# Sample attention of a hybrid decoder step: where round 1's memory rows lie, in which order round 1 is scored, and how page numbers are read

## The chip, the cores and the metric

The kernel runs on one core of a Trainium2 chip. The metric is the device time of one execution in microseconds (us), lower is better. A time stands for a kernel as the median of several runs. Engines are named as in the profile: PE is the tensor engine, PEld its weight loads, DVE the vector engine, ACT the scalar engine, POOL the GpSimd engine, SP the sync engine. SP, ACT and POOL also issue DMAs. A "q" behind an engine's name (SPq, ACTq, POOLq) stands for what its instruction sequencer does, DMA issues above all.

## What is computed

One step of a decoder layer runs over 512 prompt tokens and over 8 sample sequences of 4 new tokens each, which have 2048 past tokens in paged caches (pages of 128 tokens). Each branch of the sample attention reads a different store:

```
def sample_layer(x, cache_cmp, cache_slc, cache_win, cache_mem, pool_buf, page_table, p, rel_bias):
    ...
    full_c = jnp.concatenate([gather(cache_cmp), kvc], axis=1)
    full_s = jnp.concatenate([gather(cache_slc), kvs], axis=1)
    ...
    o_cmp, o_slc = nsa_global(q, pos, full_c, full_s, p, rel_bias)
    win_kv = jnp.concatenate([cache_win, kvw], axis=1)
    ...
    o_win = win_attention(q[:, None], pos[None, :], win_kv[:, None], kpos, rel_bias)[:, 0]
    o_nsa = nsa_combine(gn, o_cmp, o_slc, o_win)
    o_mem = mem_attention(qm, cache_mem)
    y = layer_tail(x, gb, o_pool, o_nsa, o_mem, p)
```

`gather` takes 16 pages of a sequence by its row of the page table; a page of one cache is 128 x 256 numbers of four bytes, 128 KB. The compressed branch gives the importance by which 16 of the 33 blocks of the selected branch are chosen. The prompt tokens pass through the same layer, and all tokens then pass a mixture of 32 experts.

## The kernel before, in words

The program is a row of phases. Each phase writes a separate instruction list for every engine (`with nc.Block()`); `phase_over()` puts a barrier of all engines behind it. Within a phase, engines wait for each other through semaphores, and each engine runs its list in the order written. Nothing is reordered by a scheduler.

1. The input projections of all tokens, to about 173 us.
2. The compress phase, to about 303 us. For each sample sequence s, PE multiplies the 16 pages of the compressed cache (`products(s, c)`), then makes blocks and turned keys (`blocks`, `keys`). Pages come by three issuers: SP 7 of them and ACT 3 (`load_sub`, each page through `load_page`, which reads the page number into a register and issues a DMA from there), POOL 6 (`gather_sub`, an indirect DMA that needs no register). `load_page` is line 457, its register load line 456, POOL's gather line 462. Between them PE computes five gate products that fill its time. At its end the selected pages of the first sequences are fetched already, SP's and POOL's part of them.
3. The sample attention, 304 to 382 us. The 8 sequences go in two rounds of four; the four sequences of a round lie side by side in the 128 rows of a PSUM bank. A round has kinds M (memory, 256 tokens), W_ (local window, 512 tokens), S (selected, 2048 tokens in four quarters q) and C (compressed). `BATCH` lists the score products in order, `score(n)` makes the n-th into bank n % 2, DVE adds biases and finds maxima (`quarter`, `window_max`, `memory_max`), ACT takes exponentials (`memory`, `window`, `selected`), PE turns the probabilities (`turn_memory`, `turn_window`, `turn_selected`) and multiplies them by values (`memory_rows`, `window_rows`, `selected_rows`). Those of memory put their product in a bank named "mv", those of the window "wv", those of the selected pages "sv".
4. The prompt attention, 383 to 497 us, then up-projections, the router, and the expert stage to the end.

Memory limits decide what can be loaded early. Round 0's memory rows lie in `mem_rows`, and so do round 1's memory rows (after round 0's were used), and after those round 1's window keys and values. SP waits for each: for "mv" of round 0, then loads round 1's memory; for "mv" of round 1, then loads round 1's windows. Selected pages of round 1's sequences 2 and 3 come into places that round 0's selected pages hold until "sv" of round 0. They are issued by SP, ACT and POOL (12, 8 and 12 pages); `owner` says which.

The order in BATCH before, and the semaphores behind which SP issues:

```
BATCH = [(0, M, 0), (0, W_, 0)] + [(0, S, q) for q in range(4)] + [(1, M, 0), (1, S, 0), (1, W_, 0)] + [(1, S, q) for q in (1, 2, 3)]
...
                filled(sp, 2, "mv", 0)
                for s in range(4):
                    load_memory(sp, 1, s)
...
                filled(sp, 3, "mv", 1)
                for s in range(4):
                    load_window(sp, 1, s)
```

Of the kernel before, what the change touches and what calls it, by code (L numbers as in the profile page):

```python
# [217 lines left out]
def build_program(nc, i, o, stop_after=99):  # L218

    ctx = ExitStack()  # L220
    with ctx:
# [242 lines left out]
        def load_sub(eng, s, pgs):  # L464

            for pg in pgs:
                load_page(eng, page_of(sub_buf(s), pg), "cache_cmp", s, pg, s_sub[s % 3])
# [572 lines left out]
        s_spill = sem("s_spill")  # L1040
        scr_hT = scratch("scr_hT", [128, KD * NTOK])
# [18 lines left out]
        def load_selected(eng, r, s, q, who=0):  # L1060
            for pg in range(4 * q, 4 * q + 4):
                if owner(r, s, pg) == who:
                    load_page(eng, selected_page(r, s, pg), "cache_slc", 4 * r + s, pg, s_cl[r][q])
# [39 lines left out]
        with nc.Block() as block:  # L1103
            @block.sync
            def _(sp):
# [48 lines left out]
            def _(act):  # L1154
# [33 lines left out]
                for s in range(NS):  # L1188
# [74 lines left out]
            def _(pe):  # L1263
# [80 lines left out]
                for c in range(2):  # L1344
# [21 lines left out]
        BATCH = [(0, M, 0), (0, W_, 0)] + [(0, S, q) for q in range(4)] + [(1, M, 0), (1, S, 0), (1, W_, 0)] + [(1, S, q) for q in (1, 2, 3)]  # L1366
# [10 lines left out]
                    + S_(4) + S_(5) + [(2, ("mv", 0)), (3, ("wv", 0))] + P_(0) + [(2, ("sv", 0))]  # L1377
                    + S_(6) + [(6, ("m", 1)), (3, ("mv", 1)), (6, ("o", 0)), (7, ("om", 0)), (5, ("om", 1))]
                    + S_(7) + S_(8) + S_(9) + WP_(1) + S_(10) + [(2, ("wv", 1))] + S_(11) + P_(1) + [(3, ("sv", 1)), (6, ("o", 1))])
# [22 lines left out]
        with nc.Block() as block:  # L1402
            @block.sync
            def _(sp):
# [6 lines left out]
                for s in range(4):  # L1411
                    load_memory(sp, 1, s)
# [29 lines left out]
            def _(act):  # L1442
# [64 lines left out]
                selected(0)  # L1507
                filled(act, 2, "sv", 0)
# [11 lines left out]
                window(1)  # L1520
                window_turned(1)
# [4 lines left out]
            def _(dve):  # L1526
# [165 lines left out]
                selected_turned(0)  # L1692
                selected_rows(0)
                mask_blocks(1)
                memory_max(1)
                memory_rows(1)
                quarter(7)
                window_max(1)
                quarter(9)
                window_turned(1)  # L1700
                quarter(10)
                window_rows(1)
                quarter(11)
# [5 lines left out]
            def _(pe):  # L1709
                rows_of_seq = [slice(32 * s, 32 * s + 32) for s in range(4)]  # L1710
                window_of = lambda r: mem_rows if r else win_rows
                pe.wait_ge(s_sc, 16 * 12)
# [1363 lines left out]
```

## Time and profile before

| what | value |
|---|---|
| median of 3 runs | 1854.88 us (1852.64 to 1856.59) |
| time of the profiled execution | 1856.81 us |
| its span, first to last instruction | 1854.8 us |
| mean granted PE clock over the span | 0.949 of full speed |
| PE busy | 1714.4 us, 92% of the span |
| DVE / ACT / POOL busy | 550.5 / 338.1 / 449.9 us |

A profile is one execution. "Busy" counts the time in which an engine works on an instruction; register, branch, semaphore and DMA-issuing instructions are not in it. The profiled execution is 1.93 us above the median of the three runs, so a difference found in the trace is to be put onto the median, and its own time is not the kernel's time.

### The profile page before, as it was taken

What the parts mean: (1) busy time and instruction counts of PE and PEld (TensorE: products, weight loads), DVE (VectorE), ACT (ScalarE), POOL (GpSimd) and SP (SyncE); (2) the same over time, 40 slices, a digit from 0 to 9 for tenths busy, and PEclk for the clock granted to TensorE, in tenths of its full rate; (3) what the DMA queues carried; (4) which work ended last, traced back from release to release, by engine and by line L of the source; (5) the groups of instructions that cost most, each with busy time, mean ns of one, the idle gap of its engine ahead of it and who ended that gap; (6) DMA issues with size and microseconds to landing.
All of it is one profiled execution on the core that took longest, in us unless ns stands there. A gap on an engine that the chain in (4) does not pass through costs nothing.

```text
span 1854.8 us, 40016 instructions
## 1 busy us (share of the span) xinstructions
PE 1714.4 (92%) x16080; PEld 953.3 (51%) x16080; DVE 550.5 (30%) x1391; ACT 338.1 (18%) x740; POOL 449.9 (24%) x520
## 2 busy tenths in 40 slices
PE   7998997679799999879999999999999999999992
PEld 3446785244478884534465754444444444444441
DVE  1333113446401113453232313231323232323235
ACT  3232112146400001101111111111111111111110
POOL 1122326647400006011212212221212222222220
PEclk9997997779999999879999999999999999999996
DMA  9534757850251103339999999999999999999986
GB/s 342 198 104 150 252 162 221 278 210 2 84 165 57 52 25 119 139 151 404 425 422 425 416 421 411 428 423 421 422 421 408 427 423 420 423 420 406 430 338 248
DMA packets 86641, 541.98 MB, mean 292 GB/s; under 512 B 19888, under 2 KB 44048, under 8 KB 73617
## 3 DMA queue, kind: packets, MB, share of 16 engines
q1 hardware_dynamic: 64809, 498.50, 66.8%
q0 software_dynamic: 14544, 32.03, 5.1%
q10 hardware_dynamic: 7232, 10.73, 1.8%
q8 instruction: 32, 0.52, 0.1%
q14 instruction: 24, 0.20, 0.0%
HBM read 523.39 MB, written 29.78 MB: 298 GB/s over the span
## 4 chain that ended last, share of the span: by engine, by line
PE 54%; DMA 1%; DVE 0%; issue 0%; SPq 0%; POOLq 0%; POOL 0%; ACT 0%
PE psum L2987 36%; PE psum L3013 18%; DMA arena<-y_of 1%; PE psum L2997 0%; DVE arena L2977 0%; SPq L2826 0%; SPq L2828 0%; DMA y_of<-arena 0%; DMA arena<-scr_h,arena 0%; DVE arena L2920 0%; POOL arena L2857 0%; POOLq L2788 0%; ACT arena L2906 0%; POOLq L2861 0%; POOLq L2857 0%
## 5 line engine op out<-in xcount | busy, mean ns | idle before, releaser
L2987 PE MATMUL psum<-arena 128*32 128x512 f32 x6144 | 668.2, 592 | 2.7 <-issue 2.7
L2987 PEld LDWEIGHTS psum<-arena 128*32 128x32 f32 x6144 | 234.4, 108 | 417.0 <-issue 413.3
L3013 PE MATMUL psum<-arena 128*32 128x256 f32 x6144 | 344.9, 378 | 0.0
L3013 PEld LDWEIGHTS psum<-arena 128*32 128x32 f32 x6144 | 236.0, 109 | 110.0 <-issue 9.6
L2942 DVE TENSOR_TENSOR arena<-psum,arena 128x512 f32<-128x512 f32 x96 | 66.5, 692 | 582.4 <-PE psum L2987 582.4
L2874 POOL DMA_INDIRECT y_of<-arena x96 | 97.0, 1011 | 476.2 <-ACT arena L2906 476.2
L2902 ACT ACTIVATE arena<-arena 128x256 f32<-128x256 f32 x96 | 40.1, 418 | 610.1 <-DVE arena L2944 610.1
L2618 PE MATMUL psum<-arena 128*128 128x272 f32 x608 | 144.3, 395 | 1.6 <-PEq L235 1.6
L2618 PEld LDWEIGHTS psum<-arena 128*128 128x128 f32 x608 | 116.1, 191 | 28.5 <-issue 3.3
L2853 POOL DMA_INDIRECT arena<-scr_h,arena x96 | 98.8, 1030 | 48.9 <-POOL arena L2849 28.2
L878 PE MATMUL psum<-arena 128*128 128x512 f32 (+1 forms) x256 | 97.4, 541 | 12.7 <-DMA arena<-in_w_tok 10.1
L2906 ACT ACTIVATE arena<-psum,arena 128x256 f32<-128x256 f32 x96 | 45.7, 476 | 245.7 <-PE psum L3013 245.7
L878 PEld LDWEIGHTS psum<-arena 128*128 128x128 f32 x256 | 46.1, 200 | 62.7 <-issue 60.6
L1984 POOL TENSOR_SCALAR arena<-arena 128x512 f32<-128x512 f32 (+3 forms) x64 | 68.5, 1085 | 20.0 <-DVE arena L2111 20.0
L462 POOL DMA_INDIRECT arena<-in_cache_slc,arena x60 | 59.2, 987 | 49.9 <-DMA scr_gate<-arena 26.2
L2444 DVE TENSOR_TENSOR arena<-psum,arena 128x544 f32<-128x544 f32 x24 | 17.4, 725 | 181.3 <-ACT arena L2417 174.6
L2849 POOL COPY arena<-arena 128x3 uint32 x32 | 6.1, 189 | 268.2 <-DMA y_of<-arena 238.1
L2920 DVE STREAM_TRANSPOSE arena<-arena 128x768 f32<-128x768 f32 x33 | 32.2, 977 | 120.5 <-DMA arena<-scr_h,arena 120.5
L2625 PE MATMUL psum<-arena 128*128 128x272 f32 x256 | 63.2, 398 | 3.6 <-DMA arena<-in_w_up 3.6
L462 POOL DMA_INDIRECT arena<-in_cache_cmp,arena x48 | 46.6, 970 | 76.1 <-PE psum L1298 33.8
L440 POOL CAST arena<-arena 32x8 bf16<-32x8 f32 (+1 forms) x6 | 6.2, 1033 | 240.7 <-DMA arena<-in_b_gu 219.8
L1298 PE MATMUL psum<-arena 128*128 128x256 f32 x256 | 61.2, 393 | 3.1 <-DVE arena L1232 3.1
(369 smaller groups left out, 1520.5 us busy)
## 6 DMA issues: line engine op xcount, KB each, us to landing
arena<-in_w_gu SPq DMA_DIRECT2D x64, 4096.0 KB, 15.1
arena<-in_w_down SPq DMA_DIRECT2D x32, 4096.0 KB, 14.5
arena<-in_w_gb SPq DMA_DIRECT2D x24, 512.0 KB, 4.5
arena<-y_of SPq DMA_DIRECT2D x8, 1024.0 KB, 15.3
arena<-in_cache_cmp SPq DMA_DIRECT2D x62, 128.0 KB, 3.1
arena<-in_cache_slc SPq DMA_DIRECT2D x60, 128.0 KB, 6.5
arena<-in_x_all SPq DMA_DIRECT2D x8, 512.0 KB, 11.3
arena<-in_w_tok SPq DMA_DIRECT2D x2, 2048.0 KB, 14.0
```

The lines of the kernel that those rows point to most:

```text
L462: pool.indirect_dma_start(dst, None, i[table], bass.IndirectOffsetOnAxis(page_row[:, at:at + 1], 0)).then_inc(sem, 16)
L878: mm = pe.matmul(bank(2 + c)[0:r, 0:b - a], dstT(n)[:, k], w_tok[:, k, a:b], start=(k == 0), stop=(k == KD - 1))
L1298: mm = pe.matmul(sum_bank(s, c)[:, 0:2 * n].rearrange("p (g b m) -> p g b m", g=2, b=PAGES), w_cmp[:, c, j], turned, start=(j == 0), stop= ...
L1984: ins = pool.tensor_scalar(rows, rows, c[:, g:g + 1], None, ALU.mult)
L2618: pe.matmul(bank(4 * s + h)[:, 0:HALF], w_gb[:, u % 6, k], hT[:, k, t], start=(k == 0), stop=(k == KD - 1))
L2625: mm = pe.matmul(bank(4 * s + 2 + h)[:, 0:HALF], w_up[:, k, 128 * c:128 * c + 128], oT_of(k)[:, t], start=(k == k0), stop=(k == k1 - 1))
L2853: pool.indirect_dma_start(xg[:, g], None, h_quarters, bass.IndirectOffsetOnAxis(row_from[:, g:g + 1], 0), bounds_check=4 * NTOK - 1, oob_i ...
L2874: pool.indirect_dma_start(y_quarters, bass.IndirectOffsetOnAxis(row_to[:, g:g + 1], 0), y_rows[:, g], None, bounds_check=4 * 1024 * TOPK - ...
L2906: act.activation(y_rows[:, g], dn_half(g), ACT.Copy, scale=cur_gate[:, g:g + 1]).then_inc(e_yc, 1)
L2942: dve.tensor_tensor(gu_c[:, g], gu_bank(g), bias_sb, ALU.add).then_inc(e_ba, 1)
L2987: mm = pe.matmul(gu_bank(g)[32 * j:32 * j + 32].rearrange("p (h n) -> p h n", h=2), xgT[:, g, 32 * k:32 * k + 32], gu_w(slot)[:, part, :, ...
L3013: mm = pe.matmul(dn_half(g)[32 * j:32 * j + 32], actT[:, g, 32 * k:32 * k + 32], dn_w(slot)[:, part, 256 * j:256 * j + 256], start=(k == 0 ...
```

## The change

There are four parts.

- Round 1's memory rows get a place of their own: `stripes`, the first 512 columns of each of 8 rows of 544 columns at `tail_base`, where the prompt's queries, memory queries and keys lie. Their prompt columns are first copied out to a scratch tensor in DRAM (`scr_q`, 2 MB, issued by SP in the compress phase behind the spill of `hT`), and are brought back by SP behind "mv" of round 1. PE waits for that (`s_q_again`) at the start of the prompt attention. The four memory loads themselves (2 MB) are issued by ACT near the end of the compress phase.
- With `mem_rows` free of round 1's memory, round 1's windows are loaded there behind "mv" of round 0.
- Round 1's order: memory and window first, then the four selected quarters. The parts on PE, DVE and ACT move with it. SP loads all of round 1's last selected pages behind "sv" of round 0 without a further wait.
- `load_page` becomes `load_pages`: the numbers of several pages are read with one register load. `owner` is changed so that SP's two pages of a group of four stand side by side.

```
-        def load_page(eng, dst, table, s, pg, sem):
-
-            at = PAGES * s + pg
-            first = eng.value_load(page_row[0:1, at:at + 1], min_val=0, max_val=n_rows - 128)
-            eng.dma_start(dst, i[table][bass.ds(first, 128)]).then_inc(sem, 16)
+        def first_rows_of(eng, s, pgs):
+
+            at = PAGES * s + pgs[0]
+            return nc.values_load_multi_w_load_instructions(page_row[0:1, at:at + len(pgs)], engines=[eng.engine],
+                                                            min_val=0, max_val=n_rows - 128)[1]
+
+        def load_pages(eng, dst_of, table, s, pgs, sem):
+
+            for pg, first in zip(pgs, first_rows_of(eng, s, pgs)):
+                eng.dma_start(dst_of(pg), i[table][bass.ds(first, 128)]).then_inc(sem, 16)
...
         def load_memory(sp, r, s):
-            sp.dma_start(mem_rows[:, s], i["cache_mem"][4 * r + s]
-                         ).then_inc(s_ml[s], 16)
+            dst = stripes[:, 2 * s:2 * s + 2] if r else mem_rows[:, s].rearrange("p (v c) -> p v c", v=2)
+            sp.dma_start(dst, i["cache_mem"][4 * r + s].rearrange("p (v c) -> p v c", v=2)).then_inc(s_ml[s], 16)
...
+        stripes = arena[:, tail_base:tail_base + 8 * NTOK].rearrange("p (k c) -> p k c", k=8)[:, :, 0:NP_TOK]
+        scr_q = scratch("scr_q", [128, 8, NP_TOK])
...
-                return (OF_SP, OF_ACT, OF_POOL, OF_POOL if pg // 4 % 2 else OF_SP)[pg % 4]
+                return ((OF_SP, OF_ACT, OF_POOL, OF_POOL) if pg // 4 % 2 else (OF_SP, OF_SP, OF_ACT, OF_POOL))[pg % 4]
...
                         sp.dma_start(scr_hT, hT.rearrange("p k t -> p (k t)")).then_inc(s_spill, 16)
+                        sp.dma_start(scr_q, stripes).then_inc(s_q_spill, 16)
...
+                act.wait_ge(s_q_spill, 16)
+                for n in range(4):
+                    load_memory(act, 1, n)
...
-        BATCH = [(0, M, 0), (0, W_, 0)] + [(0, S, q) for q in range(4)] + [(1, M, 0), (1, S, 0), (1, W_, 0)] + [(1, S, q) for q in (1, 2, 3)]
+        BATCH = [(0, M, 0), (0, W_, 0)] + [(0, S, q) for q in range(4)] + [(1, M, 0), (1, W_, 0)] + [(1, S, q) for q in range(4)]
...
                 filled(sp, 2, "mv", 0)
                 for s in range(4):
-                    load_memory(sp, 1, s)
+                    load_window(sp, 1, s)
                 filled(sp, 3, "wv", 0)
                 for q in range(4):
                     load_selected(sp, 1, 0, q)
                 filled(sp, 2, "sv", 0)
-                for s in range(2, 4):
-                    load_selected(sp, 1, s, 0)
-                filled(sp, 3, "mv", 1)
-                for s in range(4):
-                    load_window(sp, 1, s)
-                for q in range(1, 4):
+                for q in range(4):
                     for s in range(2, 4):
                         load_selected(sp, 1, s, q)
+                filled(sp, 3, "mv", 1)
+                sp.dma_start(stripes, scr_q).then_inc(s_q_again, 16)
...
                 selected(0)
+                memory(1)
+                window(1)
                 filled(act, 2, "sv", 0)
                 for q in range(2):
                     for s in range(2, 4):
                         load_selected(act, 1, s, q, OF_ACT)
-                memory(1)
                 memory_turned(1)
                 heads_out(0)
+                window_turned(1)
                 for q in range(2, 4):
...
             @block.tensor
             def _(pe):
+                pe.wait_ge(s_q_again, 16)
                 def queries(i_q):
```

ACT in the compress phase, behind the first sequence's blocks. In the kernel before, its list there reads as follows; lines 456 and 457 stand three times in all, once for each page, and line 1200 comes behind them.

```order
L1185 ACTIVATE arena<-psum,arena 64x2x127 x4
L456 TENSOR_LOAD arena
L456 ISA x2
L457 ISA
L457 DMA arena<-in_cache_cmp 128x256
L456 TENSOR_LOAD arena
```

The same place in the changed kernel:

```order
L1192 ACTIVATE arena<-psum,arena 64x2x127 x4
L456 TENSOR_LOAD arena
L456 ISA x6
L462 ISA
L462 DMA arena<-in_cache_cmp 128x256
L462 ISA
L462 DMA arena<-in_cache_cmp 128x256
L462 ISA
L462 DMA arena<-in_cache_cmp 128x256
L1207 DMA arena<-in_rel_bias 32x8 x4
```

One register load (TENSOR_LOAD) stands there now where three stood; the checks on the registers (ISA) and the DMAs are as many as before.

PE in the sample attention, from the turning of round 0's selected probabilities (line 1803) to the last score of round 1. Before: 1819 is `selected_rows(0)`, 1747 the memory score of round 1, 1784 and 1793 its turning and its values, 1847 and 1854 the turned rows, 1760 the window and selected scores, 1827 and 1840 `turn_window(1)` and `window_rows(1)`.

```order
L1803 MATMUL psum<-arena 128x128 x16
L1806 MATMUL psum<-arena 32x128
L1819 MATMUL psum<-arena 32x128 x68
L1747 MATMUL psum<-arena 32x256 x8
L1784 MATMUL psum<-arena 128x128 x2
L1793 MATMUL psum<-arena 32x256 x8
L1847 MATMUL psum<-arena 128x128
L1854 MATMUL psum<-arena 128x128 x4
L1760 MATMUL psum<-arena 32x512 x12
L1827 MATMUL psum<-arena 128x128 x4
L1830 MATMUL psum<-arena 32x128
L1760 MATMUL psum<-arena 32x512 x4
```

The same stretch in the changed kernel, where line 1753 is the memory score, 1825 `selected_rows(0)`, 1766 the window and selected scores:

```order
L1809 MATMUL psum<-arena 128x128 x16
L1812 MATMUL psum<-arena 32x128
L1753 MATMUL psum<-arena 32x256 x8
L1825 MATMUL psum<-arena 32x128 x68
L1766 MATMUL psum<-arena 32x512 x4
L1790 MATMUL psum<-arena 128x128 x2
L1799 MATMUL psum<-arena 32x256 x8
L1853 MATMUL psum<-arena 128x128
L1860 MATMUL psum<-arena 128x128 x4
L1833 MATMUL psum<-arena 128x128 x4
L1836 MATMUL psum<-arena 32x128
L1846 MATMUL psum<-arena 32x128 x20
```

The memory score moved ahead of `selected_rows(0)`, the window's score ahead of `turn_memory(1)`, and all four selected scores (line 1766 again, x16) now follow `window_rows(1)`.

ACT in the sample attention, behind the copies of round 0's turned probabilities. Before, it goes at once to the pages of round 1's sequences 2 and 3:

```order
L1443 ACTIVATE arena<-psum 128x512 x2
L456 TENSOR_LOAD arena
L456 ISA x2
L457 ISA
L457 DMA arena<-in_cache_slc 128x256
```

In the changed kernel three exponentials of round 1 stand ahead of them, memory (128x256) and window (128x512 and 128x32):

```order
L1450 ACTIVATE arena<-psum 128x512 x2
L1456 ACTIVATE arena<-psum,arena 128x256
L1456 ACTIVATE arena<-arena 128x512
L1456 ACTIVATE arena<-arena 128x32
L456 TENSOR_LOAD arena
L456 ISA x2
L462 ISA
L462 DMA arena<-in_cache_slc 128x256
```

ACT's first four late pages thus stand behind the window's exponential, and the other four behind `window_turned(1)`.

## Rows read from the trace of the kernel before

**Rows 1.** The page: share of the span of the chain that ended last, by engine.

```profile
PE 54%; DMA 1%; DVE 0%; issue 0%; SPq 0%; POOLq 0%; POOL 0%; ACT 0%
```

**Rows 2.** Timeline of PE, sample attention: start, duration, line, [idle before, released by].

```profile
330.76 0.42 PE L1793 MATMUL psum<-arena 128*32 128x256 f32 x4
...
335.72 4.05 PE L1819 MATMUL psum<-arena 128*32 128x128 f32 x136
343.65 1.94 PE L1747 MATMUL psum<-arena 128*32 128x256 f32 x16 [3.89 <-DMA arena<-in_cache_mem]
347.89 1.93 PE L1793 MATMUL psum<-arena 128*32 128x256 f32 x16 [0.47 <-ACT arena L1443]
...
350.02 1.30 PE L1854 MATMUL psum<-arena 128*128 128x128 f32 x4
...
361.31 1.93 PE L1760 MATMUL psum<-arena 128*32 128x512 f32 x8 [6.70 <-DMA arena<-in_win_kt]
...
368.44 1.07 PE L1760 MATMUL psum<-arena 128*32 128x512 f32 x8
...
380.86 0.33 PE L1847 MATMUL psum<-arena 128*128 128x128 f32 x1 [0.53 <-DVE arena L1658]
```

**Rows 3.** Timeline of SP's and ACT's sequencers and of ACT, sample attention.

```profile
332.05 2.28 SPq L1033 DMA_DIRECT2D arena<-in_cache_mem  x4
...
349.89 1.77 SPq L1045 DMA_DIRECT2D arena<-in_win_kt  x4
...
340.52 3.71 ACTq L457 DMA_DIRECT2D arena<-in_cache_slc  x4
...
350.95 3.77 ACTq L457 DMA_DIRECT2D arena<-in_cache_slc  x4
...
365.15 0.19 ACT L1449 ACTIVATION_READ_ACCUMULATOR arena<-arena 128x1 f32 x1
```

**Rows 4.** POOL's page gathers, 300 to 365 us: ns min/median/max, first and last start.

```profile
L462 POOL DMA_INDIRECT arena<-in_cache_slc,arena x44: 942/947/2197, 304.8 to 361.1; - x44
...
DMA to landing us min/median/max: 3.3/5.5/6.9
```

**Rows 5.** Line 457 on ACT, 350 to 355 us: issue to landing.

```profile
DMA to landing us min/median/max: 7.7/8.1/8.5
```

**Rows 6.** Stretches: busy of each engine, granted PE clock, DMA share, GB/s.

```profile
276.00:284.00 8.00, 8.00 (x42) 6.76 (x41) 1.04 (x4) 2.91 (x9) 3.78 (x4) 1.00 0.86 319
284.00:292.00 8.00, 6.94 (x55) 6.62 (x54) 2.04 (x8) 3.22 (x11) 6.12 (x7) 0.69 0.97 306
292.00:300.00 8.00, 5.46 (x29) 5.03 (x28) 0.99 (x4) 1.96 (x7) 5.24 (x6) 0.50 0.71 199
356.00:360.00 4.00, 0.00 (x0) 0.00 (x0) 0.00 (x0) 0.28 (x2) 3.02 (x4) 0.50 1.03 372
198.80:201.20 2.40, 2.40 (x7) 1.82 (x6) 0.00 (x0) 0.28 (x1) 1.78 (x2) 0.50 0.82 254
```

**Rows 7.** Timeline of ACT in the compress phase, 186 to 195 us.

```profile
186.26 2.53 ACTq L457 DMA_DIRECT2D arena<-in_cache_cmp  x3
...
194.72 0.96 ACT L1185 ACTIVATE arena<-psum,arena 64x254 f32<-64x254 f32 x2 [8.17 <-issue]
```

**Rows 8.** Timeline of PE in the compress phase: the wait, and the next gate product.

```profile
197.62 0.33 PE L1319 MATMUL psum<-arena 127*128 127x127 f32 x1 [4.22 <-DVE arena L1247]
197.78 9.19 PE L1327 MATMUL psum<-arena 128*128 128x272 f32 x32
...
230.06 7.50 PE L1327 MATMUL psum<-arena 128*128 128x272 f32 x32
```

**Rows 9.** Line 456 on ACT, 186 to 189.5 us: ns min/median/max.

```profile
L456 ACTq TENSOR_LOAD <-arena x2: 282/288/294, 186.7 to 187.7; - x2
```

**Rows 10.** Line 1103, the barrier behind the compress phase: ns, first and last start.

```profile
L1103 POOLq DRAIN  x1: 17126/17126/17126, 285.9 to 285.9; - x1
...
L1103 ACTq DRAIN  x1: 228/228/228, 300.4 to 300.4; - x1
```

More of the change, by code:

```diff
@@ L464, in load_sub @@
         def load_sub(eng, s, pgs):
-            for pg in pgs:
-                load_page(eng, page_of(sub_buf(s), pg), "cache_cmp", s, pg, s_sub[s % 3])
+            load_pages(eng, lambda pg: page_of(sub_buf(s), pg), "cache_cmp", s, pgs, s_sub[s % 3])
         def gather_sub(pool, s):
@@ L1060, in load_selected @@
         def load_selected(eng, r, s, q, who=0):
-            for pg in range(4 * q, 4 * q + 4):
-                if owner(r, s, pg) == who:
-                    load_page(eng, selected_page(r, s, pg), "cache_slc", 4 * r + s, pg, s_cl[r][q])
+            pgs = [pg for pg in range(4 * q, 4 * q + 4) if owner(r, s, pg) == who]
+            load_pages(eng, lambda pg: selected_page(r, s, pg), "cache_slc", 4 * r + s, pgs, s_cl[r][q])
         def gather_selected(pool, r, s, q):
@@ L1376, in build_program @@
                     + [(2, ("cv", 0)), (7, ("im", 0)), (3, ("cv", 1)), (7, ("im", 1))] + S_(2) + S_(3) + [(6, ("m", 0))] + WP_(0)
[L1377 to L1379 removed]
+                    + S_(4) + S_(5) + [(2, ("mv", 0)), (3, ("wv", 0))] + P_(0) + S_(6) + [(2, ("sv", 0))]
+                    + S_(7) + [(6, ("m", 1)), (3, ("mv", 1)), (6, ("o", 0)), (7, ("om", 0)), (5, ("om", 1))]
+                    + WP_(1) + [(2, ("wv", 1))] + S_(8) + S_(9) + S_(10) + S_(11) + P_(1) + [(3, ("sv", 1)), (6, ("o", 1))])
         use_no = {}
@@ L1519, in _ @@
                 memory_out(1)
-                window(1)
-                window_turned(1)
                 selected(1)
@@ L1692, in _ @@
                 selected_turned(0)
+                memory_max(1)
+                window_max(1)
                 selected_rows(0)
                 mask_blocks(1)
-                memory_max(1)
                 memory_rows(1)
-                quarter(7)
-                window_max(1)
-                quarter(9)
                 window_turned(1)
-                quarter(10)
                 window_rows(1)
-                quarter(11)
+                for n in range(8, 12):
+                    quarter(n)
                 selected_max(1)
@@ L1711, in _ @@
                 window_of = lambda r: mem_rows if r else win_rows
+                memory_of = lambda r, s, v: stripes[:, 2 * s + v] if r else mem_rows[:, s, 512 * v:512 * v + 512]
                 pe.wait_ge(s_sc, 16 * 12)
@@ L1746, in score @@
                             for s, rows in enumerate(rows_of_seq):
-                                mm = pe.matmul(bank(b)[rows, 0:MEM], qm_rows[:, mp, 4 * r + s], mem_rows[:, s, 256 * mp:256 * mp + 256],
+                                mm = pe.matmul(bank(b)[rows, 0:MEM], qm_rows[:, mp, 4 * r + s], memory_of(r, s, 0)[:, 256 * mp:256 * mp + 256],
                                                start=(mp == 0), stop=(mp == 1), tile_position=(0, 32 * s))
@@ L1792, in memory_rows @@
                         for s, rows in enumerate(rows_of_seq):
-                            mm = pe.matmul(bank(b)[rows, 0:256], pT_m[:, a, rows], mem_rows[:, s, 512 + 256 * a:768 + 256 * a],
+                            mm = pe.matmul(bank(b)[rows, 0:256], pT_m[:, a, rows], memory_of(r, s, 1)[:, 256 * a:256 * a + 256],
                                            start=(a == 0), stop=(a == 1), tile_position=(0, 32 * s))
@@ L1873, in _ @@
                 turn_selected(0)
+                score(6)
                 selected_rows(0)
-                score(6)
+                score(7)
                 turn_memory(1)
@@ L1880, in _ @@
                 turn_memory_rows(1)
-                score(7)
-                score(8)
-                score(9)
                 turn_window(1)
-                score(10)
                 window_rows(1)
-                score(11)
+                for n in range(8, 12):
+                    score(n)
                 turn_selected(1)
```

1 line of the change is left out of this document (added).

## The prediction

> **What bounds the kernel now.** I read the page's chain first [rows 1]: half of the span is PE's, and that is the expert stage, which the change doesn't touch. Whatever the change gains or loses arises before 382 us and is carried on as a shift of what follows, so I read PE's timeline over the two phases that it edits and asked at each gap what ended it.
>
> In the sample attention PE has two long waits for something that the change moves [rows 2]: 3.89 us for round 1's memory rows at 343.65 and 6.70 us for its windows at 361.31. Both follow from the single place: SP could issue memory only at 332.05 and windows only at 349.89 [rows 3]. That looks like 10 us to be had. It isn't, because a second chain runs under it. POOL issues 44 gathers from 304.8 to 361.1 us [rows 4], one every (361.1 − 304.8) / 43 = 1.31 us, so it hardly stops, and its last gather, which belongs to the last quarter, lands some 5.5 us after its start, at 366.6. The last score product begins at 368.44 [rows 2]. Removing the two waits can therefore bring that score forward by 1.8 us, and by 4.0 us if the last gather lands in the shortest 3.3 us. What follows the last score (maximum, exponential, turning, values, to 380.86) is the same work after the change.
>
> In the compress phase PE is the limit but for one gap: 4.22 us at 197.62 for DVE [rows 8], which stands behind ACT, and ACT is busy with DMA issues until 194.72 [rows 7]. The phase ends by POOL's drain at 285.9 + 17.1 = 303.1 us, while ACT is through at 300.6 [rows 10].
>
> **The change, part by part.**
>
> *One register load for several pages.* On ACT's path to the gap, three register loads become one. A load takes 288 ns [rows 9], so two fewer give 0.6 us. The other bound: three issues with their numbers take 2.53 us [rows 7], issues without numbers 1.77 / 4 = 0.44 us each [rows 3], so all that reading costs behind the first load is 2.53 − 1.32 = 1.2 us. The checks on each register stay, so I take 0.6. PE's gap shrinks by that, and the gate products, POOL's start and the barrier move forward with it. On SP the register loads have slack everywhere. In the sample attention ACT has one page per group, so nothing is saved there.
>
> The Trainium skill, "DMA: Bandwidth & Descriptors", section "Latency and other measured facts", gives a tensor_load a floor of about 600 ns; by it the two would save about 1.2 us and the sum would be 0.6 us better. The trace has 282 to 294 ns here, and I go by that.
>
> *The clock.* Behind the 4.22 us gap the granted clock is 0.50 (1.2 of 2.4 GHz) from 198.8 to 201.2 [rows 6], and that gate product takes 9.19 instead of 7.50 us [rows 8]. A gap of 3.6 us may or may not keep the upper level: 0 to 1.7 us. I take 0, since the gap stays nearer to the old one than to none.
>
> *Storing the prompt queries, 2 MB, at about 202 us.* SP issues it behind the spill of hT. The pages that follow on its queue are issued only after the next sequence's products, and PE shows no wait for a page there. I cost it at nothing.
>
> *Round 1's memory rows, 2 MB, at about 285 us on ACT.* Four issues at 0.44 us are 1.8 us on ACT just before its last copies. ACT is through 2.5 us before the barrier falls, so this is covered. The traffic is less harmless: the barrier waits for POOL's drain, which waits for the gathers to land. Between 276 and 300 us the DMA engines move 319, 306 and 199 GB/s, which is 6.6 MB in 24 us [rows 6]. With 2.1 MB more it is 8.7 MB, and at the 372 GB/s of 356 to 360 us this takes 23.4 us: no delay. By the shares instead (0.86, 0.97 and 0.71), 3.7 us are idle and the new loads need 2.1 / 0.372 = 5.6 us: 1.9 us of delay. If the gathers stood behind all of it, 5.6 us. I take 1.0, between the first two.
>
> *Windows instead of memory behind "mv" of round 0.* That bank is full at 330.76 + 0.42 = 331.2 us [rows 2]. SP, which arrived at 332.05 and saves some 12 register loads before it, is waiting by then. From the first memory issue to PE's start took 343.65 − 332.05 = 11.6 us [rows 2, 3]; four windows are as large, so PE scores them at 342.8. Meanwhile the memory score (1.07 us, as the score at 368.44) stands ahead of selected_rows(0), which ends at 335.72 + 1.07 + 4.05 = 340.8 instead of 339.8. SP's pages behind "sv" start a microsecond later, POOL's not, as its 12 last gathers only come to their turn at 361.1 − 11 × 1.31 = 346.7.
>
> *ACT's list.* Here the change adds a wait. ACT's eight late pages start at 340.52 and 350.95 now [rows 3]. In the new order the first four stand behind the window's exponential. From a window score's start to the end of its exponentials is 365.34 − 361.31 = 4.0 us [rows 2, 3], so ACT is free at 346.8; a register load and its checks take 0.7 us (from the pitch of 1.08 us in [rows 7]) and the four issues 3.7: 351.2. Then come the memory copy (0.4), memory_rows and the turned rows (347.89 to 351.32, 3.4 us [rows 2]) and the window's turning and copy (an estimate of 1.4 from the turned rows' 1.30): 356.4. The second four are issued from there, the last at about 360.5 us, ten microseconds later than before. Behind ACT's pages stand memory_turned(1) and heads_out(0), for which PE waits, but PE ends that chain before the pages are there.
>
> *The last score.* It needs POOL's last page (361.1 + 5.5 = 366.6) and ACT's last. ACT's pages landed 7.7 to 8.5 us after issue while the windows came in beside them [rows 5]; POOL's in 3.3 to 6.9 [rows 4]. At 360 us the restored queries (2 MB, issued behind SP's last page near 354) take the windows' place, but are nearly through. I take 6.5 us: 367.0, with bounds 364.4 and 369.0. The score lasts 1.07 us at the full clock (368.44) and 1.93 at half (361.31) [rows 2]; PE idles before it, so I take 1.5: it ends at 368.5 instead of 369.5. That is 1.0 us gained, within 4.0 gained and 1.4 lost.
>
> *Bringing the queries back.* Issued near 354 and as large as the windows, which took 361.31 − 349.89 = 11.4 us, they are there at about 365.5, against a need at 382. Nothing.
>
> **The sum.** −0.6 (register loads) + 1.0 (POOL's drain) − 1.0 (last score) = −0.6 us. From the profiled 1856.8 this is 1856.2. That execution is 1.9 above the median of the runs, so on their scale it is 1854.88 − 0.6 = 1854.3 us.
>
> **The rivals.**
>
> *Faster.* The clock stays up behind the shorter gap (1.7), the drain isn't delayed, and the last pages land in POOL's shortest time with PE at full clock (4.0): 0.6 + 1.7 + 4.0 = 6.3 us, 1848.6. Two of the three already give over 3.7 us. For it: there is 2 MB less between 332 and 360 us, where the engines are full (share 1.03). Against it: the restored queries put those 2 MB back before the last gather lands, and POOL's pace is unchanged.
>
> *Slower.* One mechanism, in the compress phase: the four memory loads take the DMA engines ahead of POOL's gathers, and the drain waits for all their 5.6 us. The balance is 5.6 − 0.6 − 1.0 = 4.0 us, 1858.9. It decides from a barrier 4.7 us later than now, at about 308 us. For it: the engines' share is 0.97 just where the loads start. Against it: it is 0.71 from 292 us on, so much of the delay is made good.
>
> The Trainium skill, "DMA: Bandwidth & Descriptors", section "Queues, rings and completion order", says that each DMA engine takes its queues in turn, a packet at a time; by that neither queue stands behind the other, and this rival would lose only a part of its 5.6 us. No row here shows the turns themselves.
>
> *No gain because ACT's pages become last.* They land at 369.0 and the score runs at half clock, so that it ends at 370.9 instead of 369.5: −0.6 + 1.0 + 1.4 = +1.8 us, 1856.7. This is the way in which the change wouldn't do what it says. It lies within the bound of no change.
>
> *The restored queries come late* and PE waits at the prompt attention's start. They would have to take 28 us instead of 11.4; one in a hundred, counted with slower.
>
> **How the numbers follow.** About 0.2% (3.7 us) is what a measurement can tell from no change. The forecast and the third rival lie within it: 0.58. Faster gets 0.26, as two separate uncertain terms can bring it; slower 0.16. The range from 1849.5 to 1859.0 reaches into both; the likeliest case's own range is 1852.5 to 1856.7.
>
> **What would show it.** Right: three pages on ACT at 186 us with one register load; the gap at 197.6 about 3.6 us; POOL's drain ending within 302.5 to 305; the window score of round 1 near 343; ACT's last late page near 360; the last two scores waiting for selected pages; PE starting the prompt attention without a wait. Wrong: a barrier at 308 us, a full clock at 199 us, or a last score before 365 or after 370.

## The result: 0.23% slower, and the profile after

| kernel | median of 10 runs (lowest to highest) |
|---|---|
| before | 1855.34 us (1852.64 to 1856.59) |
| changed | 1858.86 us (1856.69 to 1862.57) |

The ratio is 1.0023, 95% interval 1.0015 to 1.0031: 3.5 us on the medians. The time lies inside the range, but the forecast was no change, and it is slower. The profiled execution took 1860.03 us, its span 1858.2.

The phases, cut where the barrier lets SP go (line 235), in the first profiled execution of each kernel and in a second one of each (first two experiments):

| phase, us | before | again | changed | again |
|---|---|---|---|---|
| projections | 175.12 | 174.86 | 177.70 | 174.35 |
| compress | 128.97 | 127.51 | 129.86 | 131.65 |
| sample attention | 78.63 | 78.51 | 78.50 | 78.56 |
| prompt attention | 116.16 | 116.19 | 116.43 | 116.15 |

The 2.6 us more in the first phase of the changed kernel are those of one execution. PE's first 32 matmuls of line 940, in the timeline of the changed kernel and, below, of its second profile (which has 29 of them in this row):

```profile
154.90 6.83 PE L940 MATMUL psum<-arena 128*128 128x2 f32 x32
```

```profile
153.83 4.54 PE L940 MATMUL psum<-arena 128*128 128x2 f32 x29
```

Stretches of the first of these profiles (length, then busy us and count of PE, PEld, DVE, ACT, POOL; granted clock; DMA share; GB/s) show why:

```profile
152.00:154.00 2.00, 1.22 (x12) 0.77 (x10) 1.36 (x2) 1.38 (x10) 0.00 (x0) 1.00 0.00 1
155.00:157.00 2.00, 2.00 (x12) 2.00 (x11) 1.90 (x4) 0.39 (x1) 0.00 (x0) 0.50 0.00 0
```

The clock fell to 1.2 GHz under these matmuls there, and later in the second profile (0.70 of full speed over 155 to 157 us). Of 18 profiled executions of all kernels, 16 have a first phase of 174.3 to 175.2 us. The two long ones, this one and that of loads_alone below, both read page numbers jointly, as do 12 of the 16; the runs of loads_alone as a whole are no slower than the kernel before. That joint loads make an early fall more frequent is neither shown nor excluded.

**The compress barrier.** The lines that answer to [rows 10], POOL's and also PE's drain, and PE's in the kernel before:

```profile
L1109 POOLq DRAIN  x1: 18938/18938/18938, 287.6 to 287.6; - x1
...
L1109 PEldq DRAIN  x1: 365/365/365, 301.3 to 301.3; - x1
```

```profile
L1103 PEldq DRAIN  x1: 363/363/363, 300.0 to 300.0; - x1
```

POOL's drain takes 18.94 us instead of 17.13 and ends at 306.5, 5.2 us after PE's began; in the kernel before it was 3.1 us (300.0 to 303.1). The traffic, issue to landing of the DMAs from 278.6 to 307.6 us (the last number, us; KB each before it where it is known), and the DMA share (next to last) of the stretches that answer to [rows 6]:

```profile
arena<-in_cache_mem ACTq DMA_DIRECT2D x4, 512.0 KB, 10.0
...
arena<-in_cache_slc,arena POOLq DMA_INDIRECT x16, 6.0
```

```profile
279.50:287.50 8.00, 6.97 (x46) 5.97 (x45) 1.07 (x5) 2.89 (x8) 5.30 (x6) 1.00 1.02 370
287.50:295.50 8.00, 7.24 (x54) 7.02 (x53) 1.99 (x8) 2.40 (x10) 6.03 (x7) 0.72 1.05 362
295.50:303.50 8.00, 3.59 (x20) 3.02 (x19) 0.99 (x4) 1.53 (x6) 3.78 (x4) 0.50 0.94 313
```

The room that [rows 6] showed is used up, and POOL's gathers take 6.0 us to land. In the kernel before (276 to 306 us) it was 3.5:

```profile
arena<-in_cache_slc,arena POOLq DMA_INDIRECT x17, 3.5
```

POOL starts its gathers at the same pace in both, one every 1.25 us. From the end of its last one to the end of the drain it is 4.31 us in each of the nine profiles without memory loads beside them, the kernel before included, and 6.2 to 7.2 us in the nine with them. In all 18 the drain ends 2.7 to 3.0 us after the last packet of POOL's queue, so it is the landing that the drain waits for.

**The gap near 197 us.** ACT and PE (timelines), to set beside [rows 7, 8]. First ACT in the changed kernel:

```profile
188.60 1.33 ACTq L462 DMA_DIRECT2D arena<-in_cache_cmp  x3
...
193.40 2.69 ACTq L1210 DMA_DIRECT2D arena<-in_c_force  x1
...
196.68 0.96 ACT L1192 ACTIVATE arena<-psum,arena 64x254 f32<-64x254 f32 x2 [8.68 <-issue]
```

The issue of c_force in the kernel before, and PE's row in the changed one:

```profile
192.54 1.47 ACTq L1203 DMA_DIRECT2D arena<-in_c_force  x1
```

```profile
199.57 0.47 PE L1329 MATMUL psum<-arena 127*128 127x127 f32 x1 [4.72 <-DVE arena L1257]
199.84 8.74 PE L1337 MATMUL psum<-arena 128*128 128x272 f32 x32
```

ACT's three pages go out in 1.33 us instead of 2.53, but a later issue on the same engine, of c_force (a constant of 16.5 KB), takes 2.69 us (1.47 before), and PE's gap is not shorter but longer, 4.72 us.

**The sample attention.** PE's timeline, to set beside [rows 2] (this execution is 3.5 us later at the phase's start):

```profile
346.25 1.07 PE L1766 MATMUL psum<-arena 128*32 128x512 f32 x8 [1.95 <-DMA arena<-in_win_kt]
...
352.98 1.93 PE L1799 MATMUL psum<-arena 128*32 128x256 f32 x16 [5.30 <-ACT arena L1450]
...
363.37 0.40 PE L1836 MATMUL psum<-arena 128*32 128x128 f32 x1 [6.11 <-ACT arena L1504]
...
366.64 4.23 PE L1766 MATMUL psum<-arena 128*32 128x512 f32 x24
371.60 1.07 PE L1766 MATMUL psum<-arena 128*32 128x512 f32 x8 [0.73 <-DMA arena<-in_cache_slc,arena]
```

The two waits for memory rows and windows are gone but for 1.95 us. The time went into two new ones, 5.30 and 6.11 us, behind ACT's late pages. Three of the four selected scores then run without a wait, and the last waits 0.73 us (1.58 in the second profile) for a page that POOL gathered: it starts 64.0 us into the phase, against 64.4 before, where it followed PE's own work without a wait [rows 2]. POOL's gathers of this phase, to set beside [rows 4], have the same number and pace:

```profile
L467 POOL DMA_INDIRECT arena<-in_cache_slc,arena x44: 940/946/2337, 308.3 to 364.7; - x44
...
DMA to landing us min/median/max: 2.8/4.3/7.8
```

But the last one lands later. In the kernel before, the last two take, from start to landing:

```profile
DMA to landing us min/median/max: 5.4/5.5/5.5
```

In the changed kernel PE's wait for the last one ends 6.9 us after its start (364.7 to 371.60; 6.5 in the second profile). The restored queries, 2 MB, are under way beside it: issued at 359.81, they land 13.4 us later, and the DMA engines are full (share 1.04 to 1.05) until 370 us.

### The profile page after: what moved, and what is told of

Its sections match the earlier page's. It is cut to its first block, busy times and chain, and to the rows that moved or that the text cites. A ratio compares the mean times of both kernels' runs of the same rounds, so it can differ in the third digit from the quotient of the medians.

```text
span 1858.2 us, 39924 instructions
## 1 busy us (share of the span) xinstructions
PE 1715.0 (92%) x16080; PEld 992.7 (53%) x16080; DVE 548.6 (30%) x1391; ACT 337.5 (18%) x740; POOL 448.9 (24%) x520
## 4 chain that ended last, share of the span: by engine, by line
PE 54%; DMA 1%; DVE 0%; SPq 0%; issue 0%; ACT 0%; DVEq 0%; POOLq 0%
PE psum L2992 36%; PE psum L3018 18%; DMA arena<-y_of 1%; PE psum L3002 0%; PE psum L2352 0%; DVE arena L2982 0%; DMA y_of<-arena 0%; SPq L2831 0%; SPq L2833 0%; DVE arena L2925 0%; DVE arena L2345 0%; ACT arena L2911 0%; DVEq L2793 0%; POOLq L2883 0%; POOLq L2879 0%
## 5 line engine op out<-in xcount | busy, mean ns | idle before, releaser
L2992 PEld LDWEIGHTS psum<-arena 128*32 128x32 f32 x6144 | 261.1, 108 | 389.9 <-issue 375.4
L3018 PEld LDWEIGHTS psum<-arena 128*32 128x32 f32 x6144 | 246.7, 109 | 99.8 <-issue 8.8
```

Of the source, the lines that this page charges most:

```text
L2992: mm = pe.matmul(gu_bank(g)[32 * j:32 * j + 32].rearrange("p (h n) -> p h n", h=2), xgT[:, g, 32 * k:32 * k + 32], gu_w(slot)[:, part, :, ...
L3018: mm = pe.matmul(dn_half(g)[32 * j:32 * j + 32], actT[:, g, 32 * k:32 * k + 32], dn_w(slot)[:, part, 256 * j:256 * j + 256], start=(k == 0 ...
```

## The experiments

Ratios are against the kernel before on the same chip, with 95% intervals. "Tail" is the time from the start of PE's drain at the compress barrier to the end of POOL's drain: 3.1 us before, 5.2 us in the changed kernel.

**Both kernels again**, without an edit. 

> The kernel before, unchanged. In the profiled executions the projection phase ends at 175.12 us before and 177.70 us after, because the granted clock fell at 157.4 us there and at 154.6 us here, with the same PE rows ahead. If the place of that fall is chance of an execution, this run can show either (a phase end between 175.1 and 177.7 us); if it belongs to the kernel, it is 175.1 us again, within 0.3. The time: 1855.3 us, within 0.1% of the kernel before.

 

> The changed kernel, unchanged. If the early fall of the clock belongs to the kernel, the projection phase ends at 177.7 us again and PE's 32 matmuls that begin near 154.7 us take 6.8 us instead of 4.4; if it is chance, 175.1 us can come as well. The time: 1858.9 us, +0.2% on the kernel before.

 Measured: 0.9998 (0.9989 to 1.0007) and 1.0014 (1.0005 to 1.0024), tails 3.0 and 6.0 us. The changed kernel's first phase came out at 174.35 us: the early fall of the clock doesn't come with every execution of it.

**Single register loads**, in the changed kernel (the edit below), and **joint loads alone**, in the kernel before (the change's own edits of `load_page` and `owner`):

```
-            for pg, first in zip(pgs, first_rows_of(eng, s, pgs)):
+            for pg in pgs:
+                first = eng.value_load(page_row[0:1, PAGES * s + pg:PAGES * s + pg + 1], ...)
```

> The changed kernel, but every page number is read with a register load of its own again, also in the projection phase. Theory: the register loads cause most of the loss, through the first phase (SP is 2 to 4 us earlier there) or through DMA issues that come in tighter bursts and make ACT's later issues slower (PE's gap near 198 us is 4.7 instead of 4.2 us): then this gives back 2.5 to 3.5 us, 1855.5 to 1856.3, and the projection phase ends near 175.1 us. Rival: the loads are innocent and the 2 MB copies or chance make the difference: 1858.5 to 1859.5.

 

> The kernel before with two parts of the change alone: one register load for several pages, and the owners of the late selected pages regrouped. Theory: the register loads cause the loss, 1858 to 1859 us with a projection phase that ends near 177.7 us. Rival: they are worth nothing or a little, 1854.5 to 1855.5 us, and the loss lies in the copies of the queries, the memory rows or the new order.

 Measured: 1.0014 (1.0004 to 1.0023) and 0.9999 (0.999 to 1.0008). The times say that the loads are not the main cause; that theory fell. The profiles say that they are not free: the gap near 197 us is 4.20 us with single loads and 5.50 with joint ones.

**The stored queries alone**, in the kernel before:

```
                         sp.dma_start(scr_hT, ...)
+                        sp.dma_start(scr_q, stripes).then_inc(s_q_spill, 16)
```

> The kernel before with one part of the change alone: SP also stores the prompt queries (2 MB) behind the spill of hT, and nobody reads the copy. Theory: covered, as the prediction had it: within 0.5 us of the kernel before, POOL's drain at the compress barrier still 17.1 us and PE without a new wait for a page. Rival: the copy delays the pages behind it on SP's queue, so that PE waits and the compress phase is 0.8 to 2 us longer.

 Measured: 1.0002 (0.9993 to 1.0011), POOL's drain 17.10 us. Covered, as the prediction had it.

**Memory rows loaded elsewhere**, three times: by SP in the sample attention, by SP at the end of the compress phase, by ACT in its middle.

```
-                for n in range(4):
-                    load_memory(act, 1, n)
...
+                for s in range(4):              # mem_sample, ahead of the loads of sequence 1
+                    load_memory(sp, 1, s)
...
+                for n in range(4):              # mem_spend, behind SP's last selected page
+                    load_memory(sp, 1, n)
...
+                    if 4 <= s < 6:              # mem_early
+                        for n in range(2 * s - 8, 2 * s - 6):
+                            load_memory(act, 1, n)
```

> The changed kernel, but SP issues round 1's memory rows (2 MB) in the sample attention, behind round 0's selected pages, and no longer ACT at the end of the compress phase. Theory: those loads delay POOL's last gathers, and the drain behind which the barrier stands: without them the drain is 17.1 us again instead of 18.9 to 19.8, the barrier falls 4.0 to 4.2 us after PE is through instead of 6.1 to 7.0, and the kernel gains 2.0 to 2.6 us, unless the loads now make PE wait in the sample attention (up to 2 us for the memory score near 339 us). Rival: the drain is long for another reason (the stored queries, the order of SP's pages): then nothing changes there.

 

> The changed kernel, but SP issues round 1's memory rows behind its own selected pages at the end of the compress phase, some 10 us later than ACT did. Theory of the delayed gathers: most of the loads' packets then come behind the gathers; the drain is between 17.1 and 19 us, and the kernel gains 1 to 2.5 us. If instead ACT's issues were what cost time and not the traffic, the gain is the same with the drain still at 19 us or more.

 

> The changed kernel, but ACT issues round 1's memory rows in the middle of the compress phase (two sequences' rows each at about 248 and 260 us, where the DMA engines are a third to two thirds busy) instead of at its end. Theory: the loads beside POOL's last gathers are what makes the drain long. Then the drain is 17.1 us again, the barrier falls 4.0 to 4.2 us after PE's drain, the sample attention keeps its 78.5 us, and the kernel is 2.0 to 2.6 us faster than the changed one: 0 to +0.05% against the kernel before. Rival: the loads only move the delay to the pages of the last sequences, and PE waits there: no gain.

 POOL's drain in the three, in this order:

```profile
L1109 POOLq DRAIN  x1: 17117/17117/17117, 283.6 to 283.6; - x1
```

```profile
L1109 POOLq DRAIN  x1: 20022/20022/20022, 285.6 to 285.6; - x1
```

```profile
L1109 POOLq DRAIN  x1: 17097/17097/17097, 287.1 to 287.1; - x1
```

Ratios: 1.0016 (1.0007 to 1.0025), 1.0037 (1.0023 to 1.0051), 1.0002 (0.9993 to 1.0012). Wherever the loads are away from the end of the phase, the drain is 17.1 us again, and moved to the middle they cost nothing that the times show: 0.1 to 0.2% comes back, against the changed kernel's two ratios. SP's issue at the end is no help, against the expectation: the drain is longer still, so it is the traffic and not ACT's issues. (This version's sample attention is 2.2 us longer as well, 80.69 us.) In the sample attention the loads move the loss: the windows come late and PE waits 5.60 us for them instead of 1.95, with the phase at 83.15 us.

```profile
345.00 1.94 PE L1766 MATMUL psum<-arena 128*32 128x512 f32 x8 [5.60 <-DMA arena<-in_win_kt]
```

**What holds the last score**: ACT's copies of the memory outputs ahead of its last pages (out_first), four of POOL's late pages to SP (fewer_pool), both (out_fewer).

```
+                memory_out(0)
+                memory_out(1)
                 window_turned(1)
                 for q in range(2, 4):
...
-                return ((OF_SP, OF_ACT, OF_POOL, OF_POOL) if pg // 4 % 2 else (OF_SP, OF_SP, OF_ACT, OF_POOL))[pg % 4]
+                return (OF_SP, OF_SP, OF_ACT, OF_POOL)[pg % 4]
```

> The changed kernel with one edit: ACT copies the memory outputs out ahead of its last four late pages. Theory: PE's 6.1 us wait before the window's last turned block falls to under 1 us, but the last score still waits for POOL's last gather (start 57.2 to 57.8 us into the phase), so the phase gets only 0.5 to 2 us shorter than 78.5. Rival, that this wait alone bound the end: 3 us or more.

 

> The changed kernel with one edit: SP takes four of POOL's twelve late pages. Theory: POOL's last gather starts near 53 us into the phase, but PE still waits about 6 us before the window's last turned block and has four scores behind it, so the phase is only 0 to 1.5 us shorter than 78.5. Rival, that POOL's gathers alone bound the end, as the prediction had it: about 3.4 us shorter, as with both edits.

 

> The changed kernel with two edits in the sample attention: ACT copies the memory outputs out ahead of its last four late pages, and SP takes four of POOL's twelve late pages. Theory: in the changed kernel two things hold the last score at about 64 us into the phase, POOL's last gather, and a bank that PE waits 6.1 us for because ACT's copy stands behind ACT's pages; with both gone PE's wait before the window's last turned block is under 1 us, POOL's last gather starts near 52 us into the phase instead of 57, and the phase is 3 to 6 us shorter than 78.5. Rival: the DMA engines are full (372 GB/s), so the last pages land at the same time whoever issues them: less than 1 us.

 Ratios: 1.0024 (1.0014 to 1.0033), 0.9999 (0.999 to 1.0008), 1.0 (0.9991 to 1.0009); phases 78.88, 75.59 and 75.06 us. PE with the copies first:

```profile
354.04 0.29 PE L1836 MATMUL psum<-arena 128*32 128x128 f32 x1 [0.34 <-ACT arena L1504]
```

and with fewer pages on POOL, with POOL's gathers below:

```profile
360.59 0.40 PE L1836 MATMUL psum<-arena 128*32 128x128 f32 x1 [6.15 <-ACT arena L1504]
361.40 2.51 PE L1846 MATMUL psum<-arena 128*32 128x128 f32 x40 [0.42 <-issue]
363.85 4.84 PE L1766 MATMUL psum<-arena 128*32 128x512 f32 x32
```

```profile
L467 POOL DMA_INDIRECT arena<-in_cache_slc,arena x40: 940/946/2987, 307.2 to 359.4; - x40
```

The last scores of out_first and of out_fewer:

```profile
368.43 1.93 PE L1766 MATMUL psum<-arena 128*32 128x512 f32 x8 [1.06 <-issue]
```

```profile
364.75 1.93 PE L1766 MATMUL psum<-arena 128*32 128x512 f32 x8 [1.06 <-DMA arena<-in_cache_slc]
```

Into the phase, the last score starts at 64.0 and 64.3 us in the changed kernel's two profiles, at 63.5 in out_first, 61.1 in fewer_pool and 58.9 in out_fewer. With the 6.1 us wait taken away alone, three scores have idle times of 4.23, 2.10 and 1.06 us ahead of them instead (for pages, it seems; the profile doesn't name what ended these waits), the last of them lasts 1.93 us at half the clock (granted 0.50 over 362 to 370 us), and the phase gains nothing, against the expectation. With four gathers fewer the wait of 6.15 us stays, and all four scores follow it without a wait, the last one 3.9 us after POOL's last packet: there PE's wait for ACT is what bounds the end. That phase is 2.9 us shorter, more than expected, but its window score is already 1.1 to 1.8 us earlier than in the changed kernel, ahead of anything that the edit moves. With both edits the last score comes 5 us earlier; it runs at half the clock again, and the phase is 3.4 us shorter, as expected. So two chains that lie close together hold the last score, POOL's last page and PE's wait behind ACT's pages, and each hides what the removal of the other would bring.

**Whose joint load lengthens the gap**: single loads of the compressed pages on one engine each.

```
-            load_pages(eng, ..., s, pgs, s_sub[s % 3])
+            for group in ([[pg] for pg in pgs] if pgs is ACT_PAGES else [pgs]):     # act_single; sp_single: SP_PAGES
+                load_pages(eng, ..., s, group, s_sub[s % 3])
```

> The changed kernel, but ACT reads the numbers of its three compressed pages one by one again; SP keeps its joint load. In the runs so far with joint loads ACT's issue of the constant c_force near 193 us took 2.2 to 3.5 us and PE's gap was 4.2 to 5.5 us; with single loads on both 1.3 to 1.5 us and 3.9 to 4.2 us. Theory A: ACT's own three pages, issued within 1.3 us instead of 2.5, make its later issue wait: here the issue takes 1.3 to 1.6 us and the gap is 3.9 to 4.3 us. Theory B: SP's seven pages, issued faster, do it: the issue still takes over 2.2 us and the gap, lengthened by the single loads, is over 4.8 us.

 

> The changed kernel, but SP reads the numbers of its seven compressed pages one by one again in the compress phase; ACT keeps its joint load. Theory A (ACT's own burst): the issue of c_force takes 2.2 to 3.5 us and PE's gap near 197 us is 4.4 us or more. Theory B (SP's burst): the issue takes 1.3 to 1.6 us and the gap falls to about 3.6 us, which is what the prediction had for joint loads.

 The issue of c_force and PE's gap, ACT single:

```profile
191.71 3.11 ACTq L1211 DMA_DIRECT2D arena<-in_c_force  x1
```

```profile
198.33 0.48 PE L1330 MATMUL psum<-arena 127*128 127x127 f32 x1 [5.71 <-DVE arena L1258]
```

and SP single:

```profile
191.20 1.73 ACTq L1211 DMA_DIRECT2D arena<-in_c_force  x1
```

```profile
196.42 0.33 PE L1330 MATMUL psum<-arena 127*128 127x127 f32 x1 [3.76 <-DVE arena L1258]
```

Ratios 1.0021 (1.0012 to 1.003) and 1.0018 (1.0009 to 1.0027): the times don't tell them apart. The gaps do: it is SP's joint load (theory B). Over all 18 profiles ACT's issue of c_force takes 1.2 to 1.7 us in the six in which SP's pages are read singly, and 2.2 to 3.5 us in the twelve with joint loads on SP.

**The version with all three edits** (memory rows in the middle, copies first, fewer pages on POOL), and the same with ACT's or SP's compressed pages loaded singly. 

> The changed kernel with all three edits: memory rows in the middle of the compress phase, memory outputs copied out early, four late pages from POOL to SP. If the two causes are apart, the gains add: 2.3 us in the compress phase and 3.4 in the sample attention, so 5 to 6 us faster than the changed kernel and 2 to 3 us (0.1 to 0.17%) faster than the kernel before. If they aren't, about 0 against the kernel before.

 

> The version with the three edits (memory rows in the middle of the compress phase, memory outputs copied out early, four late pages from POOL to SP), and ACT's three compressed pages with single register loads. It was 0.22% faster than the kernel before with joint loads. By theory A 0.3 to 1 us more than that, 1850 to 1851 us; by theory B no gain, 1851 to 1852.5 us.

 

> The version with the three edits (memory rows in the middle of the compress phase, memory outputs copied out early, four late pages from POOL to SP), and SP's seven compressed pages with single register loads; ACT keeps its joint load. By theory B (SP's faster issues hold up ACT's) PE's gap near 197 us is 3.6 to 4.0 us instead of 4.65, ACT's issue of c_force takes 1.3 to 1.9 us, and the time is 0.5 to 1.5 us below that of the three edits alone, which was 0.22% faster than the kernel before: 0.25 to 0.3%. If the gap is only a matter of one execution, it is above 4.4 us again and the time within 0.3 us of the three edits alone.

 Measured:

| version | ratio (interval) | gap near 197 us |
|---|---|---|
| three edits | 0.9978 (0.9969 to 0.9987) | 4.65 us |
| and ACT single | 0.9979 (0.997 to 0.9989) | 4.92 us |
| and SP single | 0.9968 (0.9957 to 0.998) | 3.26 us |

```profile
191.42 1.20 ACTq L1211 DMA_DIRECT2D arena<-in_c_force  x1
```

All three beat both kernels. The gains of mem_early and out_fewer add, and the gap falls again with SP's single loads, below the expected 3.6 us (the row above is of that version); that its ratio is better than that of the three edits alone, the intervals don't show.

## Why the prediction was wrong, step by step

**"On SP the register loads have slack everywhere", with −0.6 for ACT's: the sign failed, on SP.** ACT's part had the right size, as far as two profiles show. The mean gap is 4.1 us in four profiles with single loads on both engines, 3.5 in two with a joint load on ACT alone (−0.6, as forecast), but 4.8 in ten with joint loads on both, and 4.9 and 5.7 with one on SP alone. PE's drain, counted from the start of the compress phase, moves alike: 124.2, 123.6, 124.9 and 126.4 us in the mean of the same groups, with up to 3.4 us between the profiles of a group. The times of the runs are too coarse for such a term. SP's sequencer shows what I left out (timelines of the changed kernel and of the one with SP single; each row holds the pages of two sequences, seven and seven):

```profile
190.06 11.14 SPq L462 DMA_DIRECT2D arena<-in_cache_cmp  x14
```

```profile
185.55 14.78 SPq L462 DMA_DIRECT2D arena<-in_cache_cmp  x14
```

A joint load lets SP issue its seven pages some 0.5 us apart instead of 1.1 (with a break of 4.6 us in the first row, until the second seven), and that burst, 190.1 to 193.2 us in the changed kernel, comes while ACT issues its constants and just ahead of c_force, on which PE's gap depends. The term measures +0.7 us, not −0.6. The slack was SP's own; I didn't ask whom a faster SP would collide with. That SP's burst lengthens ACT's issue is shown by undoing it; through what resource is not.

**+1.0 for POOL's drain: the right mechanism, too small.** In eight profiles with ACT's memory loads at the end of the phase the tail is 4.8 to 6.0 us, mean 5.4; in nine without loads there 2.2 to 3.4, mean 2.9. The term is +2.5 us; the drain alone is 19.5 us in the mean of the eight instead of 17.1. I had the bounds 1.9, by the engines' shares, and 5.6, and chose 1.0 between 0 and 1.9, with bytes over the highest rate that I found. The shares were the better guide. The slower rival had this mechanism with too high a price. The barrier at 307.6 us, near its mark, is so late partly through the clock's early fall.

The Trainium skill, "DMA: Bandwidth & Descriptors", section "Issuing engines are not separate DMA queues", says that DMAs of all issuers run on the same 16 engines and that several issuers save only issuing time. POOL's drain agrees with the first: it is longer whether ACT (18.9 to 19.9 us) or SP (20.0 us) issues the loads beside its gathers.

**−1.0 for the last score: it gained 0.3 at most.** I let POOL's last page land 5.5 us after its start, as it does in the kernel before, and gave ACT's last page 6.5. In the changed kernel ACT's last page is there 62.1 to 62.4 us into the phase, but POOL's last page takes 6.5 to 6.9 us and holds the last score until 64.0 to 64.3; in the kernel before the score starts at 64.2 to 64.4, and the phase is as long as it was. I had the restored queries there at about 365.5; they land 13.4 us after their issue instead of 11.4, at 373.2 (369.7 less the 3.5 us of this execution), so their 2 MB are under way until after the last gather's landing. That they are what delays it isn't shown: no run moves them. The other premise, that PE ends the chain behind ACT's pages before the selected pages are there, held for the last score only, by 0.7 to 1.6 us: I had missed the 6.11 us wait. The window's last turned block goes into a bank that ACT's copies of the memory outputs free, and these stood behind ACT's pages. out_first shows that this wait costs nothing as long as POOL's page comes this late, and out_fewer that it costs as soon as it doesn't.

**Right.** The window score at 342.8 (346.25 less 3.5); the stored queries at nothing, and the restored ones at nothing for the prompt attention's start; half the clock behind the gap (granted 0.50 from 199.8 to 202.2 us); ACT's late pages not the last. Two readings are off by the prediction's own rows, and neither enters the sum: ACT's last page at 360.5 would have been about six microseconds later than before, not ten (350.95 + 3.77 = 354.7), and the slower rival's barrier 5.6 − 0.6 = 5.0 us later, not 4.7.

By these sizes the sum is +0.7 + 2.5 − 0.1 (the phase) = +3.1 us; measured were 3.5 and 2.6.

## What to carry to other kernels

A wait that is removed is worth what the next chain below it leaves, and only runs that thin each chain, alone and together, show which one holds; here reordering the scores gave nothing, ACT's copies alone gave nothing, and with four of POOL's gathers moved as well the phase was 3.4 us shorter. A load that nobody waits for isn't free when an engine's drain at a barrier waits for other transfers beside it: put it where the DMA share has room, not where its issuer is idle. And when an engine with slack issues faster, look at what the other issuers send in the same microseconds.

## What the runs showed of the hardware

A register load of seven page numbers takes 0.93 us on SP, half of seven loads of one number; of three numbers on ACT it is no cheaper than three single loads. What changes most is the pitch of the issues behind, on SP 0.51 us instead of 1.10. SP's load of seven numbers in the changed kernel, and of one number in the kernel with SP single (ns, lowest, median, highest):

```profile
L456 SPq TENSOR_LOAD <-arena x3: 927/937/1116, 177.8 to 194.9; - x3
```

```profile
L456 SPq TENSOR_LOAD <-arena x20: 272/278/449, 175.0 to 198.2; - x20
```

On ACT three numbers took 709 to 1044 ns, against 282 to 294 for one [rows 9]: three singles would take some 0.87 us. The floor of about 600 ns per load of the Trainium skill ("DMA: Bandwidth & Descriptors", "Latency and other measured facts"), by which joining would have paid, is not seen for one number.

And the time of a DMA's issue is not its own: ACT took 1.2 to 1.7 us to issue the same 16.5 KB load while SP's pages came 1.1 us apart, and 2.2 to 3.5 us where they came 0.5 us apart.

A drain of POOL at a barrier lasts until its own gathers have landed: 17.1 us with room on the DMA engines, 18.9 to 20.0 us with 2 MB of other loads beside them.
